# Opening of a hybrid layer kernel: blocks of x transposed unscaled, the token factor applied after the transpose

## The chip, the cores and the metric

The kernel runs on one core of a Trainium2 chip. The metric is device microseconds of one execution. Work is spread over TensorE (PE; its weight loads are listed as PEld), VectorE (DVE), ScalarE (ACT), GpSimd (POOL) and the DMA engines, whose transfers are issued here mostly from SyncE's queue (SP) and some from GpSimd's.

## The reference, cut to what matters

One layer works on 512 prompt tokens and 64 sample tokens of width 2048. It begins with a normalisation and one wide projection:

```python
def rmsnorm(x, g):
    xf = xf * lax.rsqrt(jnp.mean(xf * xf, axis=-1, keepdims=True) + RMS_EPS)
    return (xf * g).astype(x.dtype)
...
    xn = rmsnorm(x, g_pre)
    def cols(off, width):
        return jnp.einsum('btd,dc->btc', xn, w_in[:, off:off + width])
```

Everything that follows (pooling, stick-breaking attention, mLSTM, gates, output projection, second norm) reads columns of that projection. For the opening only this counts: `xn` is needed with the 2048 channels on the partitions and the 576 tokens along the free axis, each value being x times one factor of its token (1/rms) times one factor of its channel (`g_pre`).

## The kernel before

The 576 tokens are handled as two halves of `TH` = 288. The channels are 16 groups of 128 (`KD` = 16), 8 of them (`HK`) in each of the tensors `xq[0]` (half 0, groups 0 to 7), `xq[1]` (half 0, groups 8 to 15), `xq[2]` and `xq[3]` (the same of half 1). The projection is done by seven products for a pair of 128-column tiles of `w_in` instead of eight (a Strassen-like scheme: A11, A12, S1, S2, S4, S3, A22), and the steady part multiplies in split precision: each operand has a high part and a low part, which `hi` on ACT (L1313), `lo` on DVE (L1719), and for x `x_hi` (L1347) and `x_lo` (L1761) make. The sums of x that the scheme needs (`x_s1`, `x_s2`, `x_s4`, `x_s3`) are made by `x_sum` (L1765) on DVE.

While these parts are being prepared, TensorE starts with eleven plain fp32 products, `early(0)` to `early(10)` (L862), each of 8 channel groups by 288 tokens and shown as 16 matmul records. `early(0)` needs `xq[0]` and the first weight tile `raw_11(At(0))`; `early(1)` needs `xq[1]`; `early(2)` and `early(3)` use these again with the second pair's weights; `early(6)` needs `x_s1` and a difference of weights (`tx`, `combine`, L1723). Between `early(9)` and `early(10)` stands the first split product (L854). `early(10)` must wait until DVE has read a bank (`c22_out(At(0))`, L1831), which in DVE's program order stands behind the x sums and three of the `x_lo` steps.

The x opening of the kernel before goes over five blocks of rows: four of 128 prompt tokens and one of 64 sample tokens. For each block: SyncE's queue loads it (L561, L563); ACT squares it with a row sum (`square`, L1326); DVE makes mean plus epsilon (L1735); ACT takes the root (L1331); DVE the reciprocal (L1740) and multiplies the whole block of 2048 columns by it in place (`normalise`, L1744); TensorE transposes it in four quads of four 128x128 transposes (`x_block`, L870); then each quad is copied from PSUM to `xq` with the gain: on DVE as one or two `tensor_tensor` (`x_quad`, L1752), or on ACT as four or eight activations (`x_quads`, L1339: quads 2 and 3 of block 1, all of block 3). Block 2 lies across the two halves, so its last 96 rows belong to half 1. On TensorE blocks 0, 1 and 2 are transposed before `early(0)`, block 3 between `early(0)` and `early(1)`, and block 4 behind `early(1)`.

TensorE opens with the transpose of the gain and 20 transposes of the identity into an unused bank. GpSimd issues four small loads (`vectors`, L2471: `ml_hnorm`, `pool_scale`, `b_if`, `state_ml_m`) ahead of making the identity (L2473, L2474). Their first reader on DVE is `gate_outputs`, at pair 19 of 68. SyncE's issue order is gain, x blocks 0, 1, 2, `raw_11`, x block 3, `raw_21`, x block 4, then the other weight tiles.

The order of each engine's instructions is written out by hand. The semaphores are counted: `xs_ready` (block scaled), `xtr_done` (quads transposed), `xqd_done` and `xqa_done` (quads copied by DVE and by ACT).

## Time and profile before

| what | us |
|---|---|
| median of 3 runs | 2266.11 (2265.32 to 2267.19) |
| the profiled execution: its own time | 2269.17 |
| its span (first to last instruction) | 2267.6 |
| TensorE busy in the span | 2237.9 |
| VectorE busy in the span | 1459.1 |
| granted TensorE clock, mean over the span | 0.998 |

Times in the rows are microseconds from the start of the span unless marked ns; "x16" is the number of instructions that a row merges, and what stands in square brackets is the idle time of the engine ahead of it and what ended it. L numbers are lines of the kernel before.

### The profile page before, as it was taken

The page shows a single profiled execution, that of the slowest core. Times are in us where ns is not written, and L with a number is a line of the kernel's source. Part 1 is how long each engine was busy: PE and PEld are TensorE (multiplying, and loading weights), DVE is VectorE, ACT ScalarE, POOL GpSimd, SP SyncE. Part 2 cuts the span into 40 slices and gives each one's busy share as a digit, 9 for nine tenths or more (in the row PEclk, how much of TensorE's full clock was granted, in tenths as well). Part 3 has the DMA queues.
Part 4 walks back from the last instruction along what each step waited for, and adds up shares of the span by engine and source line. Part 5 has one row for each costly group of instructions (what it writes and reads, how often), then busy time and mean ns, then how long its engine had stood idle before and what let it go on. Part 6 is the DMA issues. An engine that isn't in the chain of part 4 may idle for free.

```text
span 2267.6 us, 39882 instructions
## 1 busy us (share of the span) xinstructions
PE 2237.9 (99%) x16389; PEld 2189.0 (97%) x16389; DVE 1459.1 (64%) x1686; ACT 904.2 (40%) x1233; POOL 169.5 (7%) x224
## 2 busy tenths in 40 slices
PE   8999999999999999999999999999999999999997
PEld 6999999999999999999999999999888998999997
DVE  7876767657666666777666666665777676653234
ACT  5343433434333344444444444443654333222221
POOL 0000000000100000111000000000211122000000
PEclk9999999999999999999999999999999999999999
DMA  6443443533534444444444443436666566734443
GB/s 178 114 133 107 119 140 86 164 105 107 136 113 127 121 118 125 114 125 125 117 123 125 114 132 106 133 108 212 218 217 219 185 191 186 188 113 120 122 105 102
DMA packets 418028, 311.29 MB, mean 137 GB/s; under 512 B 11389, under 2 KB 379141, under 8 KB 416336
## 3 DMA queue, kind: packets, MB, share of 16 engines
q1 hardware_dynamic: 398720, 247.24, 39.7%
q0 software_dynamic: 18912, 61.25, 7.8%
q8 instruction: 122, 2.00, 0.4%
q10 hardware_dynamic: 240, 0.52, 0.1%
q14 instruction: 34, 0.28, 0.0%
HBM read 250.07 MB, written 58.90 MB: 136 GB/s over the span
## 4 chain that ended last, share of the span: by engine, by line
PE 95%; DVE 3%; DMA 1%; issue 1%; ACT 0%; POOL 0%; DVEq 0%; SPq 0%; ACTq 0%; POOLq 0%
PE pp L854 65%; PE pp L1055 11%; PE pp L1242 8%; PE M L870 2%; PE pp L862 1%; PE pp L1295 1%; PE M L1159 1%; PE M L1180 1%; PE M L1079 1%; PE M L1016 1%; PE M L862 1%; PE M L1108 1%; DMA out_dram<-n_out 1%; DMA out_dram<-states 0%; PE M L854 0%
## 5 line engine op out<-in xcount | busy, mean ns | idle before, releaser
L854 PE MATMUL pp<-xa,wa_hi 128*128 128x288 f32 x7392 | 1479.9, 296 | 0.6 <-DVE wa_lo L1719 0.4
L854 PEld LDWEIGHTS pp<-xa,wa_hi 128*128 128x128 f32 x7392 | 1184.7, 188 | 1.3 <-issue 0.6
L854 PE MATMUL pp<-xa,wa_lo 128*128 128x288 f32 x3696 | 1086.7, 294 | 0.0
L854 PEld LDWEIGHTS pp<-xa,wa_lo 128*128 128x128 f32 x3696 | 695.8, 188 | 0.0
L1719 DVE TENSOR_TENSOR wa_lo<-raw_a,wa_hi 128x1024 fp32r<-128x1024 f32 x262 | 326.1, 1248 | 240.8 <-ACT wa_hi L1313 240.8
L1313 ACT ACTIVATE wa_hi<-raw_a 128x1024 fp32r<-128x1024 f32 x262 | 276.6, 1056 | 203.1 <-PE pp L854 202.0
L1719 DVE TENSOR_TENSOR wa_lo<-raw_r,wa_hi 128x1024 fp32r<-128x1024 f32 x134 | 170.7, 1274 | 140.1 <-ACT wa_hi L1313 140.1
L1313 ACT ACTIVATE wa_hi<-raw_r 128x1024 fp32r<-128x1024 f32 x134 | 141.5, 1056 | 133.1 <-PE pp L854 125.8
L1055 PE MATMUL pp<-gt_hi,wb_hi 128*128 128x288 f32 x768 | 169.0, 302 | 1.7 <-DVE gz L2120 1.7
L1055 PE MATMUL pp<-gt_hi,wb_lo 128*128 128x288 f32 x768 | 164.6, 296 | 0.0
L1055 PE MATMUL pp<-gt_lo,wb_hi 128*128 128x288 f32 x768 | 164.1, 295 | 0.0
L1719 DVE TENSOR_TENSOR wa_lo<-tx_main,wa_hi 128x1024 fp32r<-128x1024 f32 x67 | 82.1, 1225 | 69.4 <-ACT wa_hi L1313 69.4
L1055 PEld LDWEIGHTS pp<-gt_hi,wb_hi 128*128 128x128 f32 x768 | 122.9, 189 | 3.6 <-DVE wb_lo L2108 1.9
L1055 PEld LDWEIGHTS pp<-gt_hi,wb_lo 128*128 128x128 f32 x768 | 123.4, 188 | 0.0
L1055 PEld LDWEIGHTS pp<-gt_lo,wb_hi 128*128 128x128 f32 x768 | 123.3, 188 | 0.0
L1723 DVE TENSOR_TENSOR raw_a<-raw_a 128x1024 f32<-128x1024 f32 x101 | 123.1, 1219 | 0.0
L2540 POOL DMA_DIRECT2D z_scratch<-zs x60 | 44.0, 733 | 1056.5 <-ACT zs L1450 583.7
L1551 ACT ACTIVATE wb_hi<-raw_b 128x1024 fp32r<-128x1024 f32 x80 | 83.8, 1052 | 50.2 <-PE pp L1242 34.6
L2108 DVE TENSOR_TENSOR wb_lo<-raw_b,wb_hi 128x1024 fp32r<-128x1024 f32 x80 | 96.4, 1221 | 11.3 <-ACT wb_hi L1551 10.9
L1242 PE MATMUL pp<-m_hi,wb_hi 128*128 128x288 f32 x448 | 97.2, 298 | 0.0
L1242 PE MATMUL pp<-m_lo,wb_hi 128*128 128x288 f32 x448 | 96.1, 295 | 0.0
L1242 PE MATMUL pp<-m_hi,wb_lo 128*128 128x288 f32 x448 | 96.1, 295 | 0.0
(324 smaller groups left out, 2153.7 us busy)
## 6 DMA issues: line engine op xcount, KB each, us to landing
raw_a<-in_w_in_dram SPq DMA_DIRECT2D x202, 512.0 KB, 5.0
raw_r<-in_w_in_dram SPq DMA_DIRECT2D x68, 512.0 KB, 5.0
z_scratch<-zs POOLq DMA_DIRECT2D x60, 576.0 KB, 3.3
raw_b<-in_w_branch_dram SPq DMA_DIRECT2D x48, 512.0 KB, 5.2
raw_b<-in_w_out_dram SPq DMA_DIRECT2D x32, 512.0 KB, 4.9
gz<-z_scratch SPq DMA_DIRECT2D x48, 288.0 KB, 5.5
qkv<-z_scratch SPq DMA_DIRECT2D x22, 288.0 KB, 5.7
gt_hi<-gated_scratch SPq DMA_DIRECT2D x4, 1152.0 KB, 7.5
```

Source lines behind the costliest of these rows:

```text
L854: i = nc.tensor.matmul(out, ws[:, slot, k, :], xa[:, o, part, k, :], start=opens and k == 0 and s == 0, stop=k == HK - 1 and s == 2, skip_ ...
L862: i = nc.tensor.matmul(out, weights[:, k, :], x[:, k, :], start=opens and k == 0, stop=k == HK - 1, skip_group_check=not opens)
L870: i = nc.tensor.transpose(out, src, ident[0:k, 0:k])
L1016: i = nc.tensor.matmul(out, wp[:, k, c * P:(c + 1) * P], pa[:, k, a:a + w], start=k == 0, stop=k == 1)
L1055: i = nc.tensor.matmul(out[:, b, :], ws[:, slot, k, :], xs_[:, k, b * TH:(b + 1) * TH], start=k == 0 and q == 0, stop=k == HK - 1 and q == 2)
L1242: i = nc.tensor.matmul(out[:, b, :], ws[:, slot, k, :], xs_[:, k0 + k, b * TH:(b + 1) * TH], start=opens and k == 0 and q == 0, stop=close ...
L1313: nc.scalar.activation(wa_hi[:, ring(n), :, :], src, ACT.Copy).then_inc(wa_hi_ready, 1)
L1551: nc.scalar.activation(wb_hi[:, n.base % RING_B, :, :], raw_b[:, n.base % RAW_B, :, :], ACT.Copy).then_inc(wb_hi_ready, 1)
L1719: nc.vector.tensor_tensor(wa_lo[:, ring(n), :, :], src, wa_hi[:, ring(n), :, :].bitcast(F32), ALU.subtract).then_inc(wa_lo_ready, 1)
L1723: nc.vector.tensor_tensor(out, a, b, ALU.subtract).then_inc(t_ready, 1)
L2108: nc.vector.tensor_tensor(wb_lo[:, n.base % RING_B, :, :], raw_b[:, n.base % RAW_B, :, :], wb_hi[:, n.base % RING_B, :, :].bitcast(F32), A ...
L2540: pool.dma_start(z_v[:, bass.ds(p.times(2).value(-16), 2), :] if p.per else z_v[:, 2 * spill_of(p.base):2 * spill_of(p.base) + 2, :], stag ...
```

## The change

Blocks of x are loaded and transposed as they land, not scaled. The factor of each token (the reciprocal root, one number per partition) is broadcast along the free axis and transposed by TensorE (`spread`), so that it lies along the tokens and is the same on all partitions; DVE copies it to SBUF (`read_scale`, `x_scale`) and each column group is then brought from PSUM to `xq` by one `scalar_tensor_tensor` that multiplies with the gain and with the token factors (`x_columns`). All of it is on DVE; ACT copies no quads any more. There are six blocks instead of five: 128, 128 and 32 rows for half 0, and 128, 128 and 32 for half 1; the two blocks of 32 rows are turned by 16 small transposes into one bank (`x_rest`). The transposes of blocks 3, 4 and 5 stand in the middle of and between `early(0)` and `early(1)` (`half_way`). Mean and epsilon move into the root's scale and bias on ACT. x block 0 is issued ahead of the gain. The identity transposes at the start are 16, ahead of the gain's, with 4 and 8 more later. The four small loads are issued behind the load of `spool`. `combine(tx(At(0)), ...)` moves on DVE from ahead of the last block's quads to behind `x_sum(x_s1)`. `x_hi(A11, ...)` waits for the end of `xq[0]` by a new count.

```diff
+X_BLOCKS = [(0, 0, P, 0, 0), (0, P, P, 0, 1), (0, 2 * P, TH - 2 * P, 0, 2),
+            (1, 0, P, 0, 3), (1, P, P, 0, 4), (1, 2 * P, TH - 2 * P, TH - 2 * P, 2)]
...
+            x_block(0)
             sp.dma_start(gpre_r[:, :], g_pre.rearrange("a (k p) -> (a k) p", p=P)).then_inc(gain_loaded, 16)
-            x_block(0)
             x_block(1)
             x_block(2)
...
+            def spread(m):
+                _, _, rows, p0, _ = X_BLOCKS[m]
+                pe.wait_ge(inverse_ready, m + 1)
+                if m:
+                    pe.wait_ge(spread_read, m)
+                nc.tensor.transpose(scale_bank[:, 0:rows], rs_x[p0:p0 + rows, m:m + 1].to_broadcast([rows, P]),
+                                    ident[p0:p0 + rows, p0:p0 + rows]).then_inc(spread_done, 1)
 
             pe.wait_ge(consts_ready, 1)
+            warm(M[:, 1536:2048], 16)
             pe.wait_ge(gain_loaded, 16)
             transposes([(M[:, 0:KD], gpre_r[:, :])]).then_inc(gain_turned, 1)
-            transposes([(M[:, 1536:1536 + P], ident[:, :])] * 20)
             pe.wait_ge(gain_ready, 1)
-            x_block(0)
-            x_block(1)
-            x_block(2)
-            pe.wait_ge(xqd_done, 4 + 2 + 2)
+            x_quad(0, 0)
+            x_quad(0, 1)
+            x_quad(0, 2)
+            x_quad(0, 3)
+            warm(scale_bank, 4)
+            spread(0)
+            x_quad(1, 0)
+            x_quad(1, 1)
+            x_quad(1, 2)
+            scaled(0, 0)
+            x_rest(2)
+            scaled(0, 1)
+            x_quad(1, 3)
+            spread(1)
+            pe.wait_ge(spread_read, 2)
+            warm(scale_bank, 8)
+            spread(2)
+
+            def third_block_begins():
+                scaled(0, 2)
+                x_quad(3, 0)
+                scaled(0, 3)
+                x_quad(3, 1)
+
+            def fourth_block_ends():
+                spread(4)
+                scaled(3, 0)
+                x_quad(4, 1)
+                scaled(3, 1)
+                x_quad(4, 2)
+                scaled(3, 2)
+                x_quad(4, 3)
+                scaled(3, 3)
+                x_rest(5)
+                spread(5)
+
+            scaled(2, 0)
             pe.wait_ge(wa_loaded[0], 16)
-            early(0, bank_a[0], raw_11(At(0)), xq[0], True)
-            x_block(3)
-            pe.wait_ge(xqd_done, 4 + 2 + 4)
-            pe.wait_ge(xqa_done, 2)
+            early(0, bank_a[0], raw_11(At(0)), xq[0], True, third_block_begins)
+            spread(3)
+            scaled(1, 3)
+            x_quad(3, 2)
+            scaled(2, 1)
+            x_quad(3, 3)
+            x_quad(4, 0)
             pe.wait_ge(wa_loaded[1], 16)
-            early(1, d_of(At(0)), raw_21(At(0)), xq[1], True)
-            x_block(4)
+            early(1, d_of(At(0)), raw_21(At(0)), xq[1], True, fourth_block_ends)
             pe.wait_ge(wa_loaded[4], 16)
+            scaled(4, 0)
             early(2, bank_a[1], raw_11(At(1)), xq[0], True)
             pe.wait_ge(wa_loaded[5], 16)
+            pe.wait_ge(spread_read, X_NB)
             early(3, d_of(At(1)), raw_21(At(1)), xq[1], True)
...
             def root(m):
-                act.wait_ge(ms_ready, m + 1)
-                nc.scalar.activation(rs_x[:, m:m + 1], ss_x[:, m:m + 1], ACT.Sqrt).then_inc(root_x_ready, 1)
+                act.wait_ge(sq_done, m + 1)
+                nc.scalar.activation(rs_x[:, m:m + 1], ss_x[:, m:m + 1], ACT.Sqrt, bias=eps, scale=1.0 / D
+                                     ).then_inc(root_x_ready, 1)
...
+            def read_scale(m):
+                half, at, rows, _, _ = X_BLOCKS[m]
+                dve.wait_ge(spread_done, m + 1)
+                nc.vector.tensor_copy(x_scale[:, half * TH + at:half * TH + at + rows], scale_bank[:, 0:rows]
+                                      ).then_inc(spread_read, 1)
+                dve.wait_ge(spread_read, m + 1)
+
+            def x_columns(m, q, tiles, bank):
+                half, at, rows, _, _ = X_BLOCKS[m]
+                for j, k in enumerate(tiles):
+                    i = nc.vector.scalar_tensor_tensor(
+                        xq[2 * half + k // HK][:, k % HK, at:at + rows], bank[:, rows * j:rows * (j + 1)],
+                        gpre_c[:, k:k + 1], x_scale[:, half * TH + at:half * TH + at + rows], ALU.mult, ALU.mult)
+                i.then_inc(xqd_done, 1)
...
+            inverse(0)
+            read_scale(0)
+            x_quad(0, 0)
+            x_quad(0, 1)
+            inverse(1)
+            x_quad(0, 2)
+            read_scale(1)
+            x_quad(1, 0)
+            inverse(2)
+            x_quad(1, 1)
+            read_scale(2)
+            x_rest(2, 0)
+            x_quad(0, 3)
+            x_quad(1, 2)
+            x_quad(1, 3)
+            inverse(3)
+            x_rest(2, 1)
+            read_scale(3)
+            x_quad(3, 0)
+            x_quad(3, 1)
+            x_quad(3, 2)
+            inverse(4)
+            x_quad(3, 3)
+            read_scale(4)
+            x_quad(4, 0)
+            x_quad(4, 1)
+            inverse(5)
+            x_quad(4, 2)
+            x_quad(4, 3)
+            read_scale(5)
+            x_rest(5, 0)
+            x_rest(5, 1)
...
             x_sum(x_s1[:, :, :], xq[2][:, :, :], xq[3][:, :, :], ALU.add)
+            dve.wait_ge(wa_loaded[0], 16)
+            dve.wait_ge(wa_loaded[2], 16)
+            combine(tx(At(0)), raw_12(At(0)), raw_11(At(0)))
```

## Rows read from the trace of the kernel before

**Rows 1.** The page: busy time of each engine over the span.

```profile
PE 2237.9 (99%) x16389; PEld 2189.0 (97%) x16389; DVE 1459.1 (64%) x1686; ACT 904.2 (40%) x1233; POOL 169.5 (7%) x224
```

**Rows 2.** Three stretches: PE, PEld, DVE, ACT, POOL busy, clock, DMA share, GB/s.

```profile
0.00:20.06 20.06, 10.62 (x70) 9.50 (x70) 10.39 (x38) 11.37 (x20) 3.88 (x11) 1.00 0.91 285
20.06:31.00 10.94, 10.94 (x65) 8.86 (x65) 6.19 (x13) 8.94 (x25) 0.00 (x0) 1.00 1.14 257
31.00:65.40 34.40, 34.40 (x153) 27.68 (x154) 33.45 (x30) 15.72 (x17) 0.51 (x1) 1.00 0.23 60
```

**Rows 3.** The chain that ended last: start, length, what.

```profile
20.06 4.15 PE pp L862 x16
24.21 1.75 PE M L870 x16
25.95 3.88 PE pp L862 x16
29.84 1.15 PE M L870 x16
30.98 7.96 PE pp L862 x32
...
65.42 3.88 PE pp L862 x16
```

**Rows 4.** Timeline of ACT, SP and POOL to 24 us: start, length, engine, line.

```profile
1.41 1.36 SPq L561 DMA_DIRECT2D xt<-in_x_prompt_dram  x3
1.46 1.07 POOL L2471 DMA_DIRECT2D hnorm<-in_ml_hnorm_dram  x1 [0.82 <-POOLq L2680]
...
4.95 0.28 POOL L2474 TENSOR_SCALAR_AFFINE_SELECT ident<-ident 128x128 f32<-128x128 f32 x1 [0.24 <-POOL ident L2473]
...
6.83 1.91 ACT L1326 ACTIVATE junk<-xt 128x2048 f32<-128x2048 f32 x1 [4.39 <-DMA xt<-in_x_prompt_dram]
...
9.05 0.20 ACT L1331 ACTIVATE small<-small 128x1 f32<-128x1 f32 x1 [0.22 <-DVE small L1735]
10.52 1.91 ACT L1326 ACTIVATE junk<-xt 128x2048 f32<-128x2048 f32 x1 [1.26 <-DMA xt<-in_x_prompt_dram]
...
22.73 1.91 ACT L1326 ACTIVATE junk<-xt 64x2048 f32<-64x2048 f32 x1 [1.56 <-DMA xt<-in_x_sample_dram]
```

**Rows 5.** The load of `raw_11(At(0))` (L580): its issue and its landing.

```profile
L580 SPq DMA_DIRECT2D raw_a<-in_w_in_dram x1: 841/841/841, 2.8 to 2.8; - x1
...
DMA to landing us min/median/max: 12.0/12.0/12.0
```

**Rows 6.** Timeline of TensorE: transposes of the identity and of block 0.

```profile
5.51 4.53 PE L870 MATMUL M<-ident 128*128 128x128 f32 x20
...
10.92 1.94 PE L870 MATMUL M<-ident,xt 128*128 128x128 f32 x16 [0.88 <-DVE xt L1744]
```

**Rows 7.** Timeline of DVE in the opening.

```profile
9.28 0.17 DVE L1740 RECIPROCAL small<-small 128x1 f32<-128x1 f32 x1 [0.27 <-ACT small L1331]
...
11.66 1.29 DVE L1752 TENSOR_TENSOR xq<-M,gpre_c 128x512 f32<-128x512 f32 x2 [0.89 <-PE M L870]
...
29.34 1.22 DVE L1723 TENSOR_TENSOR tx_start<-raw_a 128x1024 f32<-128x1024 f32 x1 [2.67 <-DMA raw_a<-in_w_in_dram]
...
31.99 2.56 DVE L1765 TENSOR_TENSOR x_s<-xq,xq 128x2304 f32<-128x2304 f32 x1
```

**Rows 8.** Timeline of DVE, later: a run of scalar_tensor_tensor, and two other operations.

```profile
130.10 0.74 DVE L1996 SCALAR_TENSOR_TENSOR sg<-M,pscale,sg 128x512 f32<-128x512 f32 x1
130.76 0.28 DVE L1998 SCALAR_TENSOR_TENSOR sg<-M,pscale,sg 128x64 f32<-128x64 f32 x1
130.95 0.74 DVE L1996 SCALAR_TENSOR_TENSOR sg<-M,pscale,sg 128x512 f32<-128x512 f32 x1
...
63.17 0.52 DVE L1831 TENSOR_TENSOR zs<-pp,s 128x224 f32<-128x224 f32 x2
...
72.21 0.27 DVE L1942 COPY state_row<-M 128x120 f32<-128x120 f32 x1
```

More of the change, by code:

```diff
@@ L583, in _ @@
             x_block(4)
+            x_block(5)
             first(At(1), column_of(1))
@@ L857, in product, with early @@
                 return i
-            def early(j, out, weights, x, opens):
+            def early(j, out, weights, x, opens, half_way=None):
                 for k in range(HK):
+                    if k == HK // 2 and half_way:
+                        half_way()
                     i = nc.tensor.matmul(out, weights[:, k, :], x[:, k, :], start=opens and k == 0, stop=k == HK - 1,
@@ L871, in transposes, with warm, scaled @@
                 return i
+            def warm(bank, times):
+                transposes([(bank[:, 0:P], ident[:, :])] * times)
             pe.sem_inc(wpool_done, 1)
-            def x_block(m):
-                rows = P if m < NT else TS
-                pe.wait_ge(xs_ready, m + 1)
-                for q in range(4):
-                    if m == 2:
-                        pe.wait_ge(xqd_done, q + 1)
-                    elif m == 3:
-                        pe.wait_ge(xqd_done, 4 + 2 + q + 1)
-                    elif m == 4:
-                        pe.wait_ge(xqa_done, 2 + q + 1)
-                    transposes([(x_bank(m, q)[:, P * j:P * j + rows],
-                                 xt[0:rows, m, (4 * q + j) * P:(4 * q + j + 1) * P]) for j in range(4)]
-                               ).then_inc(xtr_done, 1)
+            def scaled(m, q):
+                pe.wait_ge(xqd_done, X_SCALED.index((m, q)) + 1)
@@ new lines, in x_quad, with x_rest @@
+            def x_quad(m, q):
+                assert (m, q) in X_TURNS
+                pe.wait_ge(x_loaded[m], X_LOADS[m])
+                transposes([(x_bank(m, q)[:, P * j:P * (j + 1)], xt[:, X_BLOCKS[m][4], (4 * q + j) * P:(4 * q + j + 1) * P])
+                            for j in range(4)]).then_inc(xtr_done, 1)
+            def x_rest(m):
+                _, _, rows, p0, slot = X_BLOCKS[m]
+                pe.wait_ge(x_loaded[m], X_LOADS[m])
+                for k in range(KD):
+                    i = nc.tensor.transpose(x_bank(m, 0)[:, rows * k:rows * (k + 1)],
+                                            xt[p0:p0 + rows, slot, k * P:(k + 1) * P], ident[p0:p0 + rows, p0:p0 + rows])
+                i.then_inc(xtr_done, 1)
@@ L1350, in _ @@
             nc.scalar.activation(small[:, 22:23], ss_y[:, 0:1], ACT.Sqrt)
-            square(0)
-            root(0)
-            square(1)
-            root(1)
-            square(2)
-            root(2)
-            act.wait_ge(gain_ready, 1)
-            x_quads(1, (2, 3))
-            square(3)
-            root(3)
-            square(4)
-            root(4)
-            x_quads(3, range(4))
+            for m in range(X_NB):
+                square(m)
+                root(m)
             def m1_copy(p):
@@ L1742, in normalise, with inverse @@
-            def normalise(m):
-                rows = P if m < NT else TS
-                nc.vector.tensor_scalar(xt[0:rows, m, :], xt[0:rows, m, :], rs_x[0:rows, m:m + 1], None, ALU.mult
-                                        ).then_inc(xs_ready, 1)
-            def x_quad(m, q):
-                dve.wait_ge(xtr_done, 4 * m + q + 1)
-                gain = gpre_c[:, 4 * q:4 * q + 4].unsqueeze(2)
-                for h, at, a, b in x_segments(m):
-                    i = nc.vector.tensor_tensor(
-                        xq[2 * h + q // 2][:, 4 * (q % 2):4 * (q % 2) + 4, at:at + b - a],
-                        x_bank(m, q).rearrange("p (j r) -> p j r", j=4)[:, :, a:b], gain.to_broadcast([P, 4, b - a]), ALU.mult)
-                i.then_inc(xqd_done, 1)
+            def inverse(m):
+                dve.wait_ge(root_x_ready, m + 1)
+                nc.vector.reciprocal(rs_x[:, m:m + 1], rs_x[:, m:m + 1]).then_inc(inverse_ready, 1)
@@ L1757, in x_lo, with x_rest @@
+            def x_quad(m, q):
+                dve.wait_ge(xtr_done, X_TURNS.index((m, q)) + 1)
+                x_columns(m, q, range(4 * q, 4 * q + 4), x_bank(m, q))
+            def x_rest(m, q):
+                rows = X_BLOCKS[m][2]
+                dve.wait_ge(xtr_done, X_TURNS.index((m, 0)) + 1)
+                x_columns(m, q, range(HK * q, HK * (q + 1)), x_bank(m, q)[:, HK * rows * q:HK * rows * (q + 1)])
             def x_lo(o, src, x):
```

114 lines of the change are left out of this document (44 added, 70 removed).

## The prediction

> **What bounds the kernel now.** I read the page first. TensorE is busy for 2237.9 of 2267.6 us [rows 1], so only two things can shorten the kernel: less work on TensorE, or an earlier start of it. The stretches say where an earlier start could come from: up to 20.06 us TensorE is busy for 10.62 us, and from 20.06 us to 65.4 us without a break (10.94 of 10.94 and 34.40 of 34.40) [rows 2]. The chain that ended last then gives the pieces of that unbroken run: `early(0)` at 20.06 us, the 16 transposes of block 3 (1.75), `early(1)` (3.88), the 16 of block 4 (1.15), `early(2)` at 30.98, and `early(10)` at 65.42 us [rows 3]. So the opening's price is read at two marks: when `early(2)` starts, since behind it TensorE's list is the same in both kernels, and when `early(10)` starts, since that one also waits for DVE (`c22_out`). DVE is busy for 33.45 of 34.40 us between 31 and 65.4 us [rows 2]: it is a second runner hardly behind the first. Everything later is paced by TensorE and the engines that follow it; what the opening gains or loses at `early(10)` is gained or lost at the end.
>
> **The start of early(0).** Block 0 is seen by ACT at 6.83 us [rows 4]. Its load is issued one place earlier, and an issue takes 0.45 us (three in 1.36 [rows 4]), so I take 6.4. In the kernel before it is 2.62 us from there to the end of the reciprocal (6.83 to 9.28 + 0.17 [rows 4, 7]); the mean step on DVE is gone, which ACT waited 0.22 us for [rows 4], so 2.4: the reciprocal ends at 8.8. `spread(0)` is one transpose: it is 0.11 us of TensorE in a row of them (1.75/16 [rows 3]), and I give 0.4 with the way to DVE; with the copy of 128 columns from PSUM (0.27 for 120 [rows 8]) and its own wait, DVE's first scaling starts at 9.9 us. Before, with `normalise` in between, the first quad started at 11.66 [rows 7]: 1.8 us sooner.
>
> Now the price of a quad. Before, a quad is one `tensor_tensor` of 512 columns, 1.29 us for two [rows 7]. After, it is four `scalar_tensor_tensor` of 128. A run of that operation with the same operands (PSUM, a pointer scalar, SBUF) is in the trace: 512 columns to the next start 0.66 us (130.10 to 130.76), 64 columns 0.19 us (130.76 to 130.95) [rows 8]. That is 1.05 ns a column and 0.125 us for each instruction: 128 columns take 0.26 us, a quad 1.03, and 8 pieces of 32 columns 1.27. The steps up to `early(0)`, in DVE's order: quads (0,0), (0,1) to 11.95. The reciprocal of block 1 then waits for ACT: block 1 is seen at 10.52 before [rows 4]; the earlier issue and the four small loads out of the way give about 9.75, the square with its row sum and the root end at 12.1, so 12.25. Quad (0,2) to 13.3, factor copy with its wait 0.3, quad (1,0) to 14.6, reciprocal, (1,1) to 15.8, copy 16.1, the 8 small ones of block 2 to 17.35. `early(0)` starts at **17.5** instead of 20.06. Its weights landed at 2.8 + 12.0 = 14.8 us [rows 5], with fewer bytes of x ahead of them now: no bound.
>
> **From early(0) to early(2).** Before this is 10.92 us, 8.03 of matmuls and 2.90 of transposes [rows 3]. After, eight quads of transposes stand there (blocks 3 and 4) at 0.44 us: 3.5. Block 5 is 16 small ones; with half the rows of block 4's I price them by the same row, 0.07 each (1.15/16 [rows 3]): 1.1. Three spreads: 0.3. That is 4.9 us in place of 2.9, since 96 rows of half 1 were transposed ahead of `early(0)` before, and block 4 now has 128 rows. And TensorE now waits for DVE there: DVE gets the factors of block 3 only after `early(0)` (it stands ready at 21.8 and starts on block 3 at 22.9), then three quads to 26.0, so `spread(4)` waits from 25.6 to 26.2; and `spread(5)` waits for the reciprocal behind quad (4,1), from 28.75 to 29.7. Together 1.6 us. `early(2)` starts at 17.5 + 8.0 + 4.9 + 1.6 = **31.9** against 30.98.
>
> **From there to early(10).** TensorE's list is 34.44 us (30.98 to 65.42 [rows 3]): 66.3. DVE: quads (4,2) to (5,1) and the last factor copy end at 34.6, against 31.99 before, when `x_sum(x_s1)` starts [rows 7]. From that start to the end of `c22_out` it was 31.7 us (31.99 to 63.17 + 0.52 [rows 7, 8]), about 0.9 of it waiting (33.45 busy of 34.40 [rows 2]). `combine(tx)` is added, 1.22 us; it used to be free, since DVE had been idle for 2.67 us ahead of it, waiting for its weights [rows 7]. 34.6 + 30.8 + 1.2 = 66.6, so `early(10)` starts at about **66.7** against 65.42: **+1.3 us**. The two runners are 0.4 us apart, so a fault in either price up to that costs little, and beyond it is passed on whole.
>
> **The clock of TensorE.** The granted clock reads 1.00 in all slices, but the rows of instructions tell more. The 20 transposes of the identity take 4.53 us from 5.51, 0.23 us each; the 16 of block 0 take 1.94 from 10.92, 0.12 us each [rows 6], and in a stream 0.11 (1.75/16 [rows 3]): a factor of two, the lower level (1.2 GHz) and then the higher (2.4 GHz). So the rise came at about 10 us, at the end of 4.5 us of steady work. After the change block 0's quads start at about 7.0 us. If the clock rises only near 10 us again, 21 transposes stand between 7.0 and `spread(0)` (16, 4 of warming, its own): up to 10 us 14 of them are done at twice 0.11 us, the last 7 take 0.8, and DVE's start moves from 9.9 to about 11.4; 0.2 of that disappears in the wait for block 1's reciprocal: **+1.3** on all that follows, since DVE is the chain from there on. If the clock is up by 7 us, nothing is added. The warming itself starts sooner, because the identity stands behind no small loads any more: it was ready at 5.23 after 3.1 us of issues from 1.46 [rows 4], and will be at about 1.8, so the 16 transposes end at 5.2. Behind them TensorE is idle until the gain has landed, behind 1 MB of x: some 1.5 us. I take +0.9, nearer to the late rise, because of that hole.
>
> The Trainium skill's page "TensorE: Matmul & The Clock Gate", section "Part 1: The HAM clock gate", says that the lower level is the default and only sustained matmul activity releases it, and idle time gives it back. Rows 6 agree with the first half. By that rule the rise here follows the steady run that begins at 7.0 us and would come later than 10 us; the sum would then be some 3 us slower than before instead of 2.
>
> **The other edits.** The four small loads are needed at pair 19 of 68, their issue of 3.1 us on GpSimd falls behind the `spool` load, with its next load not due until some 25 us later: nothing. ACT is relieved of 24 copies (it copied six quads), but nobody waited for it: its squares wait for the loads. All of x was on the chip at 22.73 before [rows 4] with the same bytes ahead of it in the queue as now; block 5, now the last, is first wanted by TensorE at 27.6 and its factor on DVE at 29.5: nothing. The two 32-row loads of x move 256 KB each; if each took double its share of time, block 2 would land 0.7 us later than I count, about 11, still before ACT is free for it at 12.1.
>
> **The sum.** +1.3 and +0.9 is **+2.2 us**. The profiled execution: span 2267.6 + 2.2 = 2269.8, its own time 2269.17 + 2.2 = 2271.4. The median of the runs stands 3.1 below that execution's time, so 2266.1 + 2.2 = **2268.3 us**.
>
> **Bounds.** The quad: 0.64 us (the old one of 512 columns) to 1.2 (each instruction at 0.30). At 0.64, and an early clock, `early(0)` starts at 16.5, `early(2)` at 29.2, and all is 2.0 faster than before; at 1.2 with a clock at 10 us, 5.8 slower. The clock: from 0 to +2.7 (all of blocks 0, 1 and 2 at the lower level). Loads 0.5 sooner or later: 0.5 either way.
>
> **The rivals.**
> - *The earlier start is kept* (10%). Quads cost about what they did and the clock is up: `early(0)` starts 3.5 us sooner, at 16.5, gives 2.0 back to the added transposes (4.9 for 2.9), wins and loses half a microsecond in waits, and ends 2.0 ahead at 65.4 us: 2264.1. For it: the loads do land by then. Against it: the 0.19 us that 64 columns cost [rows 8].
> - *The clock stays low into early(0)* (6%, slower by more than 0.2%). TensorE rests several times before `early(0)`, up to 2.5 us at a time, where it waits for DVE. If it is at 1.2 GHz there, `early(0)` takes 8 us instead of 4, and the transposes ahead of it have cost +2.7: 1.3 + 2.7 + 4 = 8, so 2274. It decides from the point where the rise comes later than about 14.5 us. Against it: before, TensorE was idle for 9.4 of the first 20.06 us [rows 2], most of it in rests between the blocks, and block 3's transposes still took 0.11 us each [rows 3].
> - *A gain above 0.2%* (2%). It would need more than 4.5 us, more than the whole of the 3.5 that the loads allow, so it needs something in the long rest to shift.
> - *The forecast*, between 0.5 and 4.5 us slower (82%): 2266.6 to 2270.6.
>
> What a measurement of this kernel can tell from no change is 0.2%, 4.5 us. The first rival and the forecast lie both within it. Faster 0.02, same 0.91, slower 0.07 (the low clock, and 1 in 100 from the dear end of the quad). The range 2264.9 to 2270.6 leaves out the fast end of the first rival and the low clock.
>
> **What would show the steps.** In the profile after: scalar_tensor_tensor of 128 columns 0.26 us apart; the first scaling at 10 to 11 us; `early(0)` at 17.5 to 18.8; `early(2)` 1 to 2.5 us later than 30.98, with waits of TensorE for DVE of about 1.6 us in between; `early(10)` right behind `c22_out`. Transposes of block 0 at 213 ns would confirm the clock term. The prediction is wrong if DVE takes these operations in half the time, if DVE's list has more rest before `early(10)` than I counted, or if the rest of the kernel does not keep the shift.

## The result, and the profile after

The changed kernel takes 2274.56 us (median of 10 runs, 2269.83 to 2282.65); the kernel before, on the same chip, 2266.94 (10 runs, 2265.32 to 2268.78). The ratio is 1.0032, with a 95% interval of 1.0024 to 1.004: slower, and by more than a measurement of this kernel leaves in doubt. The prediction was 2268.3 within 2264.9 to 2270.6, with 0.91 on no difference and 0.07 on slower. Two things stand out before any row is read: the middle of the runs lies 7.6 us above before, and the runs are spread over 12.8 us where those of before are spread over 3.5.

The profiled execution of the changed kernel took 2269.83 us, the shortest of its ten; its span is 2268.1, half a microsecond more than that of the trace of before, which was itself taken in an execution 3.1 us above the median of its runs. So it shows the change at its best, with the clock of TensorE high from 4.8 us to the kernel's last stage (2257.6 us). First the page's busy times of the kernel after, then three stretches of it (columns as in [rows 2]).

```profile
PE 2240.5 (99%) x16419; PEld 2191.0 (97%) x16419; DVE 1467.8 (65%) x1762; ACT 900.8 (40%) x1212; POOL 169.2 (7%) x224
```

```profile
0.00:16.77 16.77, 10.79 (x80) 9.49 (x81) 8.43 (x55) 10.57 (x14) 0.84 (x7) 1.00 0.93 293
16.77:31.05 14.28, 13.10 (x83) 10.70 (x84) 13.41 (x58) 7.00 (x9) 0.00 (x0) 1.00 1.11 263
...
31.05:65.79 34.74, 34.62 (x155) 27.61 (x153) 34.67 (x45) 15.07 (x17) 3.58 (x5) 1.00 0.23 56
```

TensorE has 2.6 us more work than in [rows 1]. `early(0)` starts at 16.77 instead of 20.06 [rows 2], and from there to `early(2)` TensorE has rests that it had not before (13.10 of 14.28 us). Next the timeline of DVE and that of TensorE, kernel after.

```profile
8.39 0.16 DVE L1786 RECIPROCAL small<-small 128x1 f32<-128x1 f32 x1 [1.80 <-ACT small L1401]
9.19 0.29 DVE L1791 COPY x_scale<-pp 128x128 f32<-128x128 f32 x1 [0.64 <-PE pp L920]
9.52 2.16 DVE L1798 SCALAR_TENSOR_TENSOR xq<-M,gpre_c,x_scale 128x128 f32<-128x128 f32 x8
...
33.87 2.56 DVE L1821 TENSOR_TENSOR x_s<-xq,xq 128x2304 f32<-128x2304 f32 x1
```

```profile
1.72 3.46 PE L890 MATMUL M<-ident 128*128 128x128 f32 x16 [1.72 <-POOL ident L2531]
...
6.64 1.97 PE L890 MATMUL M<-ident,xt 128*128 128x128 f32 x16 [0.27 <-DVE gpre_c L1782]
...
16.77 2.21 PE L882 MATMUL pp<-xq,raw_a 128*128 128x288 f32 x8 [2.28 <-DVE xq L1798]
...
25.59 0.32 PE L920 MATMUL pp<-ident,small 128*128 128x128 f32 x1 [0.43 <-DVE small L1786]
...
29.07 0.24 PE L920 MATMUL pp<-ident,small 32*128 32x32 f32 x1 [0.75 <-DVE small L1786]
...
31.29 7.92 PE L882 MATMUL pp<-xq,raw_r 128*128 128x288 f32 x32
```

Eight of the new operations take 2.16 us, 0.27 each (priced 0.26 in the prediction). TensorE waits 2.28 us ahead of `early(0)` for DVE. Behind it stand two short waits, 0.43 ahead of `spread(4)` and 0.75 ahead of `spread(5)` (priced together at 1.6), and `early(2)` starts at 31.29. `x_sum(x_s1)` starts at 33.87 against 31.99 [rows 7]. In the chain that ended last, `early(10)` stands right behind `c22_out`:

```profile
65.30 0.45 DVE zs L1887 x2
65.74 0.04 issue
65.79 4.15 PE pp L882 x16
```

65.79 against 65.42 [rows 3]: with a high clock the whole new opening costs 0.4 us in this execution. So the other 7 us of the medians are not in this trace, and had to be looked for in other executions.

### The profile page after: what moved, and what is told of

The parts are those of the page before. It is cut to its first block, busy times and chain, and to the rows that moved or that the text cites. A ratio compares the mean times of both kernels' runs of the same rounds, so it can differ in the third digit from the quotient of the medians.

```text
span 2268.1 us, 40017 instructions
## 1 busy us (share of the span) xinstructions
PE 2240.5 (99%) x16419; PEld 2191.0 (97%) x16419; DVE 1467.8 (65%) x1762; ACT 900.8 (40%) x1212; POOL 169.2 (7%) x224
## 4 chain that ended last, share of the span: by engine, by line
PE 92%; DVE 3%; DMA 1%; issue 1%; ACT 0%; POOL 0%; DVEq 0%; SPq 0%; ACTq 0%; POOLq 0%
PE pp L872 65%; PE pp L1125 11%; PE pp L1312 8%; PE M L890 2%; PE pp L1365 1%; PE M L1229 1%; PE M L1250 1%; PE M L1149 1%; PE M L1086 1%; PE M L1178 1%; DMA out_dram<-n_out 1%; DMA gt_lo<-gated_scratch 1%; PE M L872 0%; PE M L1018 0%; DVE xa L1817 0%
```

## The experiments

Each result is the median of a kernel, with its lowest and highest run; "before" beside it is the kernel before in the same session. The mark used for the opening is the start of `early(10)` in the chain that ended last: 65.42 us before [rows 3], 65.79 in the trace above. The times at which the granted clock rises and falls are those of the clock's record in each trace. Except in the six cut kernels (e10 to e13, e18, e19) nothing of the computation is left out.

**e1_after_again and e9_after_third: the changed kernel as it is.**

> The changed kernel as it is. Theory A (the clock): in its one profiled execution the work of the opening cost only 0.4 us more than before at early(10), while the ten runs spread over 13 us and their mean granted clock went down with the time (0.998 at 2268.1 us of span, 0.993 at 2281.0). So in most executions TensorE's clock is lowered for some time in the opening, where TensorE works in short pieces with rests. A expects times spread over 2270 to 2283 us again, the clock below 0.998 wherever the time is above 2271, and, in the trace if this one is a slow one, transposes or early matmuls at twice their length between 5 and 40 us. Theory B (the late small loads, or anything later in the kernel, make it slow): the time is lost behind 45 us, with the matmuls of the opening at full pace.

> The changed kernel once more, for another trace: in both traces so far the clock of the opening stayed high (early(10) at 65.8 us), while 16 of 18 runs were slower than that leads one to expect. Theory A: in this trace, if its time is above 2272, the clock is at its lower level for some time between 12 and 40 us and early(10) starts 2 to 8 us later than 65.8. Theory B (a later stage): early(10) at 65.8 again.

e1: 2272.03 us (2269.67 to 2274.88, 8 runs), before 2266.3; ratio 1.0026 (1.0016 to 1.0037). The trace of e1 is of an execution of 2273.08 us, and its opening is as good as that of the trace above: the clock rises at 4.85 us and does not fall, and the mark is at 65.82. What it loses, it loses behind the mark, where the granted clock is 0.50 in two stretches (rows in the last section). e9 is a single run of 2279.51. Its timeline of TensorE, its stretches and its chain:

```profile
1.72 3.67 PE L890 MATMUL M<-ident 128*128 128x128 f32 x16 [1.72 <-POOL ident L2531]
...
6.80 3.67 PE L890 MATMUL M<-ident,xt 128*128 128x128 f32 x16 [0.27 <-DVE gpre_c L1782]
...
18.89 4.21 PE L882 MATMUL pp<-xq,raw_a 128*128 128x288 f32 x8 [2.27 <-DVE xq L1798]
```

```profile
10.88:17.71 6.83, 4.92 (x46) 4.05 (x44) 6.29 (x27) 4.98 (x9) 0.00 (x0) 1.00 1.07 329
17.71:24.54 6.83, 5.65 (x16) 4.40 (x17) 5.55 (x29) 3.62 (x4) 0.00 (x0) 0.50 1.09 247
...
34.77:38.19 3.42, 3.42 (x9) 2.39 (x8) 3.38 (x20) 0.00 (x0) 0.00 (x0) 0.50 0.20 54
```

```profile
72.24 3.88 PE pp L882 x16
```

Most of what this execution loses is lost here. The granted clock is 0.50 from 17.71 to 24.54 us and again from 34.77 to 38.19: the lower level, 1.2 GHz. The 16 transposes of block 0 take 3.67 us instead of 1.97, and the first half of `early(0)` 4.21 instead of 2.21. The mark is at 72.24, 6.4 us later than in the trace above, and it adds up to within 0.2: the late rise (10.88 us instead of 4.81) moves `early(0)` by 18.89 - 16.77 = 2.1; the two low stretches hold 5.65 + 3.42 = 9.07 us of TensorE's work, half of which, 4.5, is lost. Against the trace of before the span is 10.2 us longer, 6.8 of it at the mark and 3.4 behind it. Note the order: the clock was up for 6.8 us and then fell, in the 2.27 us in which TensorE waits for DVE ahead of `early(0)`.

**e2_filled and e7_filled_all: TensorE kept at work in its rests**, with transposes of the identity that nobody reads.

```diff
-            warm(M[:, 1536:2048], 16)
+            warm(M[:, 1536:2048], 21)
...
             spread(2)
+            scaled(0, 2)
+            warm(M[:, 1024:1536], 20)
```

e7 has these and, in `fourth_block_ends`, 6 more ahead of `spread(4)` and 9 ahead of `x_rest(5)`.

> The changed kernel with TensorE's rests filled: 21 instead of 16 transposes of the identity ahead of the gain, and 20 more into an unused bank between spread(2) and early(0), where it waited 2.3 us for VectorE. Theory A: the clock is no longer lowered, so the spread shrinks to that of the kernel before (about 3 us) and the median is 0.4 to 1.5 us above it: 2267.3 to 2268.5. Theory B: nothing changes, 2272 to 2277 with the same spread.

> The changed kernel with the fills of the earlier run (21 at the start, 20 ahead of early(0)) and two more where its clock was still lowered at 30.4 us: 6 transposes ahead of spread(4) and 9 ahead of the 16 small ones of block 5, in banks that are free there. The path of VectorE is not touched. Theory A: median 2266.3 + 0.4 to 1.5, so about 2267.5, spread 4 us. If it stays at 2270 like the run with the first two fills, the rest of the loss does not come from the clock in the opening.

e2: 2270.31 (2268.62 to 2274.25, 11 runs), before 2266.3, ratio 1.002 (1.0011 to 1.0029). e7: 2271.71 (2266.76 to 2273.32, 11 runs), before 2267.69, ratio 1.0017 (1.0008 to 1.0026). In the trace of e7 the opening is at the high level from 6.55 us on and the mark is at 66.08; the time is still 4.0 us over before. e2 lies between its two theories, e7 well above its own (2267.5). The trace of e2 did lose the clock in the opening: not at the filled rest ahead of `early(0)`, but from 30.36 to 33.78 us, behind the two short rests ahead of `spread(4)` and `spread(5)` that e2 leaves unfilled, and its mark is at 67.62:

```profile
29.51 3.40 PE L882 MATMUL pp<-xq,raw_a 128*128 128x288 f32 x8
```

In the trace of the changed kernel these 8 take 2.21 us. So filling did what it should in the opening of e7, and part of the loss is elsewhere: the granted clock of both traces also has a low stretch between 1883 and 1891 us.

**e3_small_first: the four small loads back ahead of the identity.**

```diff
+            for dst, src in vectors:
+                pool.dma_start(dst, src, allow_slow_non_contiguous=True).then_inc(vectors_loaded, 16)
             steps.begin(0, 1)
...
             pool.dma_start(spool[:, :], state_pool[0, 0, :, :]).then_inc(spool_loaded, 16)
-            for dst, src in vectors:
-                pool.dma_start(dst, src, allow_slow_non_contiguous=True).then_inc(vectors_loaded, 16)
```

> The changed kernel with the four small loads back where they were, ahead of the identity. The identity is then ready at about 5 us, so the 16 transposes run until 8.5 and the gain's and block 0's come behind them without a rest. Theory A: the start of everything is later by 1 to 2 us, and since TensorE's first run of work is longer and without the rest at 5 to 6 us, the clock is lowered more seldom: the median somewhere between 2268 and 2275, not clear. Theory B with the small loads as the cause: back to about 2267 to 2268 with a small spread.

2274.61 (2273.82 to 2277.33, 5 runs), before 2266.3; ratio 1.0035 (1.0022 to 1.0049). The moved loads are not the cause; with them in their old place it is worse. The identity is ready at 5.29 us again, the clock rises at 11.28, `early(0)` starts 3.7 us later than in the trace of the changed kernel, and then the clock falls just the same, here 1.1 us into `early(0)`; the mark is at 72.72. Two stretches and a row of TensorE:

```profile
21.52:24.93 3.41, 3.41 (x12) 2.73 (x11) 3.31 (x17) 0.37 (x1) 0.00 (x0) 0.50 1.03 163
...
35.17:38.59 3.42, 3.42 (x9) 2.40 (x8) 3.38 (x19) 0.00 (x0) 0.00 (x0) 0.50 1.08 288
```

```profile
20.45 3.19 PE L882 MATMUL pp<-xq,raw_a 128*128 128x288 f32 x8 [2.28 <-DVE xq L1798]
```

**e5_before_loads and e6_before_loads_filled: the moved loads alone, in the kernel before.** Block 0 ahead of the gain, the small loads late, 36 transposes of the identity ahead of the gain's.

```diff
-            sp.dma_start(gpre_r[:, :], g_pre.rearrange("a (k p) -> (a k) p", p=P)).then_inc(gain_loaded, 16)
             x_block(0)
+            sp.dma_start(gpre_r[:, :], g_pre.rearrange("a (k p) -> (a k) p", p=P)).then_inc(gain_loaded, 16)
...
+            transposes([(M[:, 1536:1536 + P], ident[:, :])] * 36)
             pe.wait_ge(gain_loaded, 16)
             transposes([(M[:, 0:KD], gpre_r[:, :])]).then_inc(gain_turned, 1)
-            transposes([(M[:, 1536:1536 + P], ident[:, :])] * 20)
```

e6 has 10 more of them ahead of block 0 and 18 between blocks 0 and 1.

> The kernel before with three of the edits alone: x block 0 is issued ahead of the gain, the four small loads are issued behind the spool load, and the transposes of the identity (36 of them, since they can now start at 1.7 us) stand ahead of the gain's. Theory A: block 0 lands 0.9 us sooner and nothing else changes, TensorE works without a rest up to the gain, so 0.5 to 1 us faster than before, 2266.0 to 2266.5, with a small spread. If the late small loads are the cause (B), this one is slow too: above 2270.

> The kernel before with the earlier block 0, the small loads late (as the run before it of this kind), and TensorE's two longest rests of that run filled with transposes of the identity: 10 behind the gain's and 18 between blocks 0 and 1, where it rested 2.2 us and the clock went to the lower level at 15.3 us. Theory A (short rests in the opening lower the clock in some executions): the run without the fill had a median of 2267.6 and a spread of 8.7 us; with it the spread falls to that of the kernel before, 4 us, and the median to 0.9 us below it (block 0 is seen 0.9 us sooner): 2265.4. If the fill does nothing, 2267.6 again.

e5: 2267.61 (2263.67 to 2272.39, 11 runs), before 2266.3, ratio 1.0006 (0.9996 to 1.0015). Its median is that of before, but its runs are spread over 8.7 us. Its timeline of TensorE shows that the old order of work can lose the clock too (from 15.26 to 18.67 us), here with an early rise (at 5.01 us):

```profile
14.23 2.75 PE L870 MATMUL pp<-ident,xt 128*128 128x128 f32 x16 [2.20 <-DVE xt L1744]
17.07 2.73 PE L870 MATMUL M<-ident,xt 128*128 128x128 f32 x16
```

Blocks 1 and 2 take 2.75 and 2.73 us against 1.97 in the trace of before. At the mark this fall cost nothing, 65.12 against 65.42, so the spread of e5 is not explained by it. e6: 2271.5 (2266.1 to 2275.98, 11 runs), before 2267.69, ratio 1.0013 (1.0004 to 1.0022). That was a miss, since 2265.4 was expected: filling made it slower, though its opening is at the high level from 7.32 us on and its mark is at 65.32. The waits between 1940 and 1972 us and a stretch of its trace say where:

```profile
ACT m_hi L1655 <- DMA out_dram<-n_out: 20.4, 1, 20.4
...
PE pp L1057 <- DVE gz L2122: 6.1, 1, 6.1
```

```profile
1966.57:1973.40 6.83, 4.62 (x19) 4.65 (x20) 6.59 (x9) 3.73 (x6) 0.00 (x0) 0.50 0.51 143
```

ACT's copy `m_hi(0)` waits for the landing of a store of 4 KB, `n_out`; behind ACT stand DVE and TensorE, which rests 6.1 us, and then the clock is low for 6.8 us. The same waits in the kernel before:

```profile
ACT m_hi L1653 <- DMA out_dram<-n_out: 17.4, 1, 17.4
...
PE pp L1055 <- DVE gz L2120: 1.7, 1, 1.7
```

**e8_before_again: the kernel before, one run.**

> The kernel before once more, for a second trace: its first profiled execution took 2269.2 us, 2.9 more than the median of its runs. Theory A: early(10) starts at 65.4 us again and the clock is at its higher level from about 10 us to the last stage; what differs between executions lies in the stretch from 1760 to 1985 us.

2267.36; the clock is high from 9.67 us to 2255.6, when TensorE's work is done, the mark at 65.19, and TensorE rests 1.3 us for `gz` at 1961.

**e10, e11, e12, e13: the opening by itself.** Four kernels are cut off behind the 68 pairs: attention, mLSTM, the branch products and the output are left out, on every engine. e10 is the kernel before, e11 the changed one, e12 is e7 cut, e13 is e6 cut.

```diff
             product(At(product_at(PAIRS).base), bank_a[1], A22, False).then_inc(wa_used, 1)
+            return
```

> The kernel before, cut off behind the last of the 68 pairs: attention, mLSTM, the branch products and the output are left out and the outputs are not written. In the traces so far nothing shifts between 100 us and 1700 us, so the time of this kernel is the opening plus a constant, free of what the later stages add. Both theories: some 1500 us, a spread of 1 to 2 us. It is the base for the three cut kernels that follow.

> The changed kernel with the same cut. Theory A (the clock in the opening): a wide spread, from 0.4 us above the cut kernel before (clock high throughout) to 7 us and more (low for 10 us of the opening as in the slow trace), with a median 3 to 6 us above. Theory B (the loss is mostly in a later stage): 0.4 to 1 us above in nearly all runs.

> The changed kernel with all fills, cut: its whole form had a median of 2271.7 in spite of the fills, and in its trace early(10) was hardly late. Theory A: the fills hold the clock, so 0.5 to 1.5 us above the cut kernel before, spread below 2 us; what is left of the loss in the whole kernel is then made in the stage behind 1760 us. If it is 4 us above, the fills do not hold the clock.

> The kernel before with the loads' order, the small loads late and the fills, cut. Block 0 is seen 0.9 us sooner, so 0 to 0.9 us below the cut kernel before, spread below 2 us. Its whole form was slower than before by 3.8 us in the median, though in its trace the opening was 0.1 us ahead and 7 us were lost between 1760 and 1985 us: if this cut form is level with the cut kernel before, that loss lies in the later stage and comes from where the clock's rises and falls come to lie there, not from the opening's work.

Five runs of each: e10 1595.65 (1595.29 to 1596.29), e11 1598.07 (1596.48 to 1598.93), e12 1596.36 (1596.33 to 1597.89), e13 1596.06 (1595.03 to 1597.15). The opening alone costs 2.4 us by these medians, which is between the two theories of e11, and 0.7 with its rests filled (e12); e13 shows that e6 lost next to nothing ahead of the later stage. In all traces of cut kernels the span behind the mark is 1528.7 to 1529.1 us, so what the opening loses at the mark is lost at the end of the pairs.

The median of e12 hides that filling does not always hold the clock. Two of its five runs took 1597.9, and one of these is its trace: the granted clock falls at 13.86 us, though TensorE had rested for no longer than 0.45 us at a time since 7 us, and stays low to 17.28. The 20 transposes of the fill, 2.40 us in e2, and the mark:

```profile
14.97 3.51 PE L892 MATMUL M<-ident 128*128 128x128 f32 x20
...
67.22 4.15 PE pp L884 x16
```

By the mean the filled opening costs 1.2 us.

**e14 to e17: the wait for the `n_out` store moved**, and with it the wait for the last `states` stores. What the `n_out` store reads is first written over by `m_lo(9)`, so `m_hi(8)` can wait instead of `m_hi(0)`.

```diff
+                if t == KD // 2:
                     act.wait_ge(state_stored, 32 * MLH)
                     act.wait_ge(n_stored, 32)
```

> The kernel before with one wait moved: ACT's copy m_hi(0) of the branch stage waits for the landing of the n_out and states stores (12.0 to 16.1 us after their issue in ten traces), though their memory is first written over with m_lo(9). Now m_hi(8) waits for them. In both traces of the kernel before TensorE rests behind this wait at about 1961 us (1.7 and 1.35 us). Both theories: that rest goes, the kernel is 1.4 to 1.7 us faster, 2264.5 to 2265.

> The changed kernel with the same wait moved. Theory W: what the whole changed kernel loses beyond the 2.4 us of the cut one comes from this wait, whose rest of TensorE is longer there (2.3 to 2.8 us in four of its traces, 1.35 to 1.7 before) and at times ends in a stretch at the lower clock (3.4 us long in two of them). Then the distance to e14 falls to 2 to 3 us, about 2267, and the runs lie closer together. Theory C: it comes from the clock in any of the rests at 1881, 1901 and 1961 us; then two of the three stay, and the distance to e14 remains 4 to 5 us, about 2269.5.

> All rests of the changed opening filled with transposes that nobody reads (as e7), and the wait moved. Cut off behind the pairs the filled opening cost 0.7 us more than the kernel before, whole 4.0. Theory W: 0.5 to 1.5 us behind e14, about 2265.5. Theory C: still 3 to 4 us behind e14, about 2268.5.

> The kernel before with block 0 ahead of the gain and the small loads late (as e5, within 0.1% of before), and the wait moved. Theory W: level with e14, 2264 to 2265.5. Theory C: between e14 and 1.5 us slower than it.

11 runs of each, before 2267.22 (33 runs):

| kernel | us | ratio to before | over before, without the move |
|---|---|---|---|
| e14: before, wait moved | 2265.39 (2264.41 to 2266.62) | 0.999 (0.9981 to 1.0) | 0 |
| e15: after, wait moved | 2269.28 (2267.09 to 2273.32) | 1.0011 (1.0002 to 1.002) | e1: 5.7 |
| e16: e7, wait moved | 2268.65 (2266.24 to 2270.65) | 1.0006 (0.9997 to 1.0015) | e7: 4.0 |
| e17: e5, wait moved | 2266.01 (2264.66 to 2269.16) | 0.9996 (0.9987 to 1.0005) | e5: 1.3 |

The rest at 1961 us is gone from all four traces. The kernel before gains 1.8 us, the changed one 5.7 - 2.1 = 3.7, e7 2.6 and e5 2.5: the wait cost the kernels with another opening more. But e15 is still 3.9 us behind e14, and e16 3.3. Neither theory fits alone: the distances are nearer to theory C's, but in none of the four traces is the clock low between the opening and the last stage. In the chain of e15 another store's landing decides at 1901 us, where TensorE rests for 2.0; in e14 the same store lands sooner and TensorE rests there for 0.4 only. First e15, then e14:

```profile
1895.88 5.18 DMA out_dram<-states
```

```profile
1893.59 3.64 DMA out_dram<-states
```

The early landing is not the old opening's doing by itself: in the trace of the kernel before this store took 5.48 us, and TensorE rested 2.3 us behind it. The four traces also say how much of the distance is the opening's. The marks are at 66.08 (e14), 67.44 (e15), 65.81 (e16) and 65.15 (e17); from the mark to the end of the span it is 2197.7, 2200.1, 2202.2 and 2198.4 us. So of the 3.8 us between the spans of e15 and e14 only 1.4 lie ahead of the mark, and e16, whose mark is 0.3 us ahead of that of e14, loses 4.5 behind it. It loses them in rests of TensorE, of which e14 has 0.7 for `mk_lo`, 1.0 for `W_ml` and none for `gt_lo`:

```profile
PE M L1282 <- DVE W_ml L2391: 2.5, 1, 2.5
PE M L1254 <- DVE mk_lo L2354: 2.1, 2, 2.0
PE pp L1129 <- DMA gt_lo<-gated_scratch: 1.1, 1, 1.1
```

**e18 and e19: e10 and e11 once more.**

> The kernel before, cut off behind the 68 pairs, once more, so that the price of the opening alone has twice as many runs: 1595.65 the first time. Both theories: 1595 to 1596.5.

> The changed kernel, cut off behind the 68 pairs, once more: 2.4 us behind the cut kernel before the first time, with runs from 1596.48 to 1598.93. With the wait for the n_out store moved the whole changed kernel still stands 3.9 us behind (e15 against e14). Theory O (the opening costs 3 to 4 us by itself, and the first reading of 2.4 was low): 1598.5 to 1600. Theory S (the opening costs 2.4 us, and 1.5 us arise at the landings of other stores at about 1754 and 1901 us): 1597.5 to 1598.5.

e18 1595.78 (1595.31 to 1596.24, 5 runs); e19 1602.43 (1597.51 to 1602.87, 5 runs), beyond what either theory gave. All ten runs of each together: the cut kernel before lies between 1595.3 and 1596.3, mean 1595.7; the cut changed one between 1596.5 and 1602.9, mean 1599.6. So the opening costs 0.8 to 7.2 us by the execution and 3.9 in the mean (3.6 by the spans, since some of these executions took up to 1.2 us more outside the span than the others). That is the distance of e15 from e14 too, but in the traces of those two only 1.4 us of it lie ahead of the mark, so the match may be chance. Stretches, timeline of TensorE and chain of e19:

```profile
12.46:15.84 3.38, 1.33 (x9) 0.98 (x9) 3.31 (x17) 2.73 (x5) 0.00 (x0) 1.00 1.16 330
```

```profile
15.84:22.66 6.82, 6.08 (x17) 4.76 (x18) 5.11 (x26) 2.79 (x6) 0.00 (x0) 0.50 1.04 243
...
32.91:36.32 3.41, 3.41 (x9) 2.42 (x8) 3.38 (x20) 0.00 (x0) 0.00 (x0) 0.50 0.67 180
```

```profile
14.07 0.24 PE L922 MATMUL pp<-ident,small 32*128 32x32 f32 x1
16.58 4.21 PE L884 MATMUL pp<-xq,raw_a 128*128 128x288 f32 x8 [2.27 <-DVE xq L1802]
```

```profile
70.16 3.88 PE pp L884 x16
```

Here the rise was early (5.60 us), `early(0)` starts even before that of the trace after (16.58), and still the mark is 4.4 us later: the clock fell at 15.84, when TensorE had been busy for 1.33 of the last 3.38 us, and 6.08 + 3.41 = 9.5 us of its work stand in low stretches, of which half, 4.7, is lost.

All traces of the two openings as they are, side by side, in us:

| trace | clock rises at | low in the opening | mark |
|---|---|---|---|
| before | 10.07 | never | 65.42 |
| before (e8) | 9.67 | never | 65.19 |
| before (e10) | 11.01 | never | 65.26 |
| before (e14) | 14.57 | never | 66.08 |
| before (e18) | 10.48 | never | 65.04 |
| changed | 4.81 | never | 65.79 |
| changed (e1) | 4.85 | never | 65.82 |
| changed (e11) | 4.89 | never | 65.51 |
| changed (e15) | 10.10 | never | 67.44 |
| changed (e19) | 5.60 | 15.84 to 22.67, 32.91 to 36.32 | 70.16 |
| changed (e9) | 10.88 | 17.71 to 24.54, 34.77 to 38.19 | 72.24 |

e15 is the late rise alone, the event that the prediction had priced: block 0's transposes at the lower level and the mark 1.65 us later than in the trace of the changed kernel.

```profile
6.63 3.64 PE L890 MATMUL M<-ident,xt 128*128 128x128 f32 x16 [0.27 <-DVE gpre_c L1783]
```

## Why the prediction was wrong

**What held.** The price of the new operation (0.26 predicted, 0.27 measured); the start of DVE's scaling (9.9, measured 9.52); `early(0)` at 17.5 (16.77); 1.6 us of waits between `early(0)` and `early(2)` (0.43 + 0.75 = 1.18 measured, and `early(2)` at 31.29 where 31.9 was said); `early(10)` right behind `c22_out`; moved loads at nothing (e3, e5). The first term of the sum, +1.3, measures +0.4 where the clock is high, since DVE is 0.7 us ahead of its list (`x_sum(x_s1)` at 33.87 where 34.6 was said). A late rise was priced at +1.3 and measures +1.65 (e15). What the prediction said of DVE's work is right to a microsecond. The first rival's terms (3.5 less 2.0, the waits even) come to 1.5 us where it says 2.0; it did not occur, so nothing hangs on it.

**The step that failed is the clock's term**, "+0.9", with its bounds "from 0 to +2.7 (all of blocks 0, 1 and 2 at the lower level)". It knew one event, a late rise, and priced it in the blocks' transposes only. The runs show a second one: in some executions the clock, once risen, falls again, in the 2.3 us in which TensorE waits for DVE ahead of `early(0)` and again near `spread(5)`, and then `early(0)`, the transposes behind it and the start of `early(2)` are done at half speed. It measures +4.4 us at the mark in e19 and, with a late rise as well, +6.4 in e9. Where +2.2 was forecast for the whole opening, it costs 3.6 us by the spans of ten cut executions (3.9 by their times), and 2.4 in the mean of the six traces of the table against the five of before; 0.4 of that is the first term.

**The rival had the place and the wrong condition.** "The clock stays low into early(0)" was priced at 8 us, 2274, and given 6%, since it was said to decide only "where the rise comes later than about 14.5 us". In e19 the rise came at 5.6 us. The argument against it was that before TensorE was idle for 9.4 of its first 20.06 us, "most of it in rests between the blocks", and block 3's transposes still took 0.11 us each. That reading is wrong: 5.3 of the 9.4 us stand ahead of TensorE's first instruction, and only 4.2 between the blocks. And it was one trace of one kernel: e5, with the same order of work as before, lost the clock in blocks 1 and 2. That the result, 2274.56, is the rival's 2274 is luck: its 8 us were all to be lost in the opening, behind a rise so late that no trace of the changed kernel has it. The rule of the Trainium skill that the prediction named (page "TensorE: Matmul & The Clock Gate", section "Part 1: The HAM clock gate": idle time gives the clock back) agrees with e9 and e19 in its direction, but it is not all that the runs show: the same rests left the clock high in four other traces, and in e12 it fell while TensorE was hardly idle. The prediction used the rule for the time of the rise alone. It did see the rests ahead of `early(0)`, "up to 2.5 us at a time", but let them matter only where the rise was late.

**The second step that failed**: "what the opening gains or loses at early(10) is gained or lost at the end". Up to the end of the pairs this held (the cut kernels), behind them not. With the same opening and the wait for `n_out` moved, the changed kernel stands 2.1 us over before instead of 5.7, and e1, whose mark is only 0.4 us late, takes 3.5 us more from the mark to the end than the trace of before. A landing that ACT waits for at 1961 us takes 12.0 to 16.1 us in ten traces, TensorE rests behind it for up to 6.1 us, and in five of the ten it then works at the lower level for 3.4 to 6.8 us. The kernel before loses there too, 1.8 us by e14, and the others 2.5 to 3.7.

**The sum as measured.** Of the 5.7 us by which e1 is over before, 1.8 are what the wait for `n_out` costs the changed kernel (3.7) beyond what it costs before (1.8). The other 3.9, the distance of e15 from e14, are the opening's in part: the opening costs 2.4 to 3.9 us in the mean, by the three ways of counting above, but in the traces of e15 and e14 1.4 us stand ahead of the mark and 2.4 behind it, in longer rests at 1901 us and after. How the mean of the runs divides between the two is not shown. In the first measurement the distance was 7.6; the 1.9 between the two measurements of the same kernel (10 and 8 runs) was not explained by a trace, and with runs spread over 12.8 us it may be chance.

**What stays open.** Why one execution of the same kernel keeps the clock and the next does not: the trace after and e19 have the same list of work up to `early(0)`, to 0.2 us up to the rest ahead of it, and only one of them falls. Nor is it shown why the wait at 1961 us costs more behind another opening, at equal marks; in e6 against e8 the `n_out` store itself took 16.1 us instead of 12.7. And e16 is 3.3 us behind e14, though its cut twin e12 was only 0.7 behind e10: its trace puts the loss behind the mark, in rests for `W_ml`, `mk_lo` and `gt_lo`, the second behind a `states` store of 5.18 us; what lengthens the first, which is 2.5 us in e7 too and 1.0 in the traces of before, stays open. The wait at 1901 us was not moved.

**A version that is ahead of both, if barely**: e14, the kernel before with one wait moved, 2265.39 us against 2267.22; its interval ends at 1.0, so the gain is at the edge of what these runs can tell. The new opening is not in it.

## What to carry to other kernels

An earlier start that leaves TensorE at rest for 2 us just ahead of its first long run of matmuls can cost more than it gives, since that run is then at times done at half speed: price each new rest not only by its length but by the work that stands behind it. Filling the rests seems to help (cut off behind the pairs, 1.2 us in the mean of five runs filled, 2.2 and 5.5 in two times five unfilled), but it is no guarantee (e12). One trace of an opening says little about the clock; look at the spread of the runs first (3.5 us before, 12.8 after), and profile more than one execution before forming a theory. When two kernels differ, compare the traces at a mark as well as at the end: an equal distance in two pairs of kernels (3.9 us here) need not lie in the same place. And look at what a counted wait protects: the one for `n_out` stood eight copies ahead of where the memory was needed, and it made a 4 KB store decide the time.

## What the runs showed of the hardware

The two levels alternate more finely than the slices of a page of the profile show: the PEclk rows of e1 and e9 read 9 throughout, while their granted clock is 0.50 for stretches of 3.4 and 6.8 us, in the opening (e9) and at 1903 and 1968 us, as here in e1. Each of these two stretches begins while TensorE is back at work behind a rest of 2.0 and 2.5 us.

```profile
1902.66:1906.07 3.41, 3.41 (x5) 1.34 (x6) 3.20 (x4) 0.16 (x1) 3.41 (x4) 0.50 0.08 18
1967.51:1970.93 3.42, 3.42 (x16) 3.42 (x16) 3.39 (x6) 1.59 (x3) 0.00 (x0) 0.50 0.92 258
```

A store of 4 KB of non-contiguous columns (`n_out`) took 12.0 to 16.1 us in the chains of ten traces, while the stores of 256 KB on the same queue (`states`) took 3.6 to 5.5. It is issued right behind two of those; how much of its time is spent behind them was not told apart.
